# Both MLPs by seven products per 2x2 block, and a pooling mixer in ten overlapping tiles

## The chip, the cores and the metric

The kernel runs on one core of a Trainium2 chip, in fp32. TensorE multiplies, VectorE, ScalarE and GpSimd work element by element, SyncE issues most transfers. The metric is device time in microseconds; the kernel before took 2031.56 us (median of 3 runs, 2031.04 to 2033.41).

## The reference

One inference step of a two-layer decoder trunk, for a prompt of 1024 tokens behind 16 learned meta tokens, and for 8 samples of 4 tokens, which share the weights: 1072 tokens in all, 1024 channels.

```python
def sqrelu_mlp(x, w_up, w_down):
    return jnp.square(jax.nn.relu(x @ w_up)) @ w_down

# layer 0: h = rmsnorm(x); z = h @ w_in_even  -> gated short convolution (width 3)
#          and sliding-window attention with sinks -> concat @ w_out_even -> + x
# layer 1: h = rmsnorm(x); pool_mix(h): per channel group of 256 a trailing mean over
#          2 / 4 / 8 / 16 tokens minus h, times w_pool[group], times pool_scale -> + x
# both:    x = x + sqrelu_mlp(rmsnorm(x, norm_mlp[layer]), w_up[layer], w_down[layer])
```

`w_up` is 1024 x 4096 and `w_down` 4096 x 1024 per layer. The outputs are the activations of prompt and samples and the states of convolution, attention cache and pooling. The meta tokens are not needed after the mixer, so the second MLP works on 1056 tokens.

## The kernel before

Activations lie transposed in the state buffer: `xT` (named residual) holds 8 chunks of 128 channels by 1072 tokens. An fp32 product is made of three fp32r products: each operand is split into a high part (`_hi`, a copy on ScalarE) and a low part (`_lo`, a subtraction on VectorE), and `product` (L451 to L455) issues high x high, high x low and low x high into one PSUM bank. Columns are tokens in pieces of 368, 352 and 352; weights are the stationary 128 x 128 operand.

The stages follow one another: input projection, attention woven into the convolution's projections, the output projection in two halves of the contraction (`w_out_half`), the first MLP, the pooling mixer, the second MLP. An MLP runs over 8 groups of 512 hidden channels. In each group `up` makes 12 outputs of 24 matmuls, VectorE and ScalarE turn them into the hidden values (`relu`, `sq`, `hid_hi`, `hid_lo`) in the state buffer, and `down` makes 24 outputs of 12 matmuls, which VectorE adds to the residual (L1424). Four PSUM banks rotate. Weights come in steps of 512 KB through `raw` (two buffers) and are split into four slots of `w_hi` and `w_lo`.

The norm before an MLP needs a mean over channels: ScalarE squares, VectorE sums four chunks at a time (`norm_reduce`), a matmul sums over partitions, then root and reciprocal (`norm_rsqrt`). The up matmuls take the residual times the gain; `rs`, the factor per token, comes in with `relu`. So the matmuls of the first MLP do not wait for the norm. The mixer maps each of nine tiles of 128 tokens through `w_pool` (`map_tile`), scales the result (`z`), and makes the windows by a matmul with a band matrix (`window_tile`), one for the tile's own tokens and a second, 16 columns wide, for the tile before.

The order on each engine is the order in which the code is written; engines wait on one another by counting semaphores. GpSimd only issues transfers.

## Time and profile before

| | |
|---|---|
| median of 3 runs | 2031.56 us |
| profiled execution | 2034.41 us |
| its span, first to last instruction | 2032.6 us |
| first MLP | 447.6 to 1206.6 us |
| pooling mixer | 1206.6 to 1282.5 us |
| second MLP | 1282.5 to 2029.2 us |
| mean granted TensorE clock | 0.986 of full |

The profile's busy time of TensorE counts matmuls that overlap in the pipeline, so a matmul's mean duration is about twice the distance between two starts. What a stream of matmuls costs is read from the starts.

### The profile page before, as it was taken

Reading aid. Unit: us, or ns where it says so; the run is one execution under the profiler, and the core shown is the slowest. Engines: PE = TensorE matmul, PEld = TensorE weight load, DVE = VectorE, ACT = ScalarE, POOL = GpSimd, SP = SyncE. Lnnn points to the kernel's source line nnn. Section 1 sums busy time; section 2 is a strip of 40 time slices with the busy share of each in tenths; the row PEclk is TensorE's granted clock in tenths of the full one; section 3 lists DMA queues with packets and bytes.
Section 4 is the critical chain, followed back from the end, with each engine's and each line's share of the span. In section 5 each row is a group of like instructions: output and inputs, shape, how many; then the busy total and the mean of one; then the engine's idle time right before and its main releaser. Section 6 shows DMA issues by size and latency. Waiting matters only on the chain.

```text
span 2032.6 us, 30057 instructions
## 1 busy us (share of the span) xinstructions
PE 1989.8 (98%) x12287; PEld 1945.2 (96%) x12287; DVE 961.5 (47%) x1595; ACT 522.9 (26%) x929; POOL 36.2 (2%) x72
## 2 busy tenths in 40 slices
PE   5999999999999999999999999999999999999999
PEld 4888888999999999999999999999999999999999
DVE  5777775484333333333433477643433333334333
ACT  4323333143121221212131342312131212212120
POOL 1010000100000000000000000000000000000000
PEclk8899999999999999999999998899999999999999
DMA  5311101311111110211111110011111111112112
GB/s 178 84 49 32 32 32 59 99 42 61 43 42 42 41 55 28 62 31 51 52 42 51 43 42 5 21 52 53 52 40 53 41 41 41 41 41 62 31 53 86
DMA packets 134887, 102.01 MB, mean 50 GB/s; under 512 B 4481, under 2 KB 132657, under 8 KB 134784
## 3 DMA queue, kind: packets, MB, share of 16 engines
q1 hardware_dynamic: 130880, 90.52, 14.6%
q0 software_dynamic: 3648, 10.39, 1.7%
q8 instruction: 52, 0.85, 0.2%
q14 instruction: 19, 0.16, 0.0%
q10 hardware_dynamic: 288, 0.09, 0.0%
HBM read 95.17 MB, written 6.09 MB: 50 GB/s over the span
## 4 chain that ended last, share of the span: by engine, by line
PE 91%; DVE 5%; ACT 2%; issue 1%; DMA 1%; SPq 0%; DVEq 0%; ACTq 0%
PE out L453 29%; PE out L455 28%; PE out L454 28%; PE out L817 2%; PE turned L630 1%; DVE norm_sum L1158 1%; DVE head_sq L1214 1%; DMA raw<-in_w_in_even 1%; PE turned L613 1%; PE turned L509 1%; PE scores L579 1%; DVE w_lo L1148 0%; DVE act_lo L1181 0%; DVE rs L1173 0%; DVE conv_y L1367 0%
## 5 line engine op out<-in xcount | busy, mean ns | idle before, releaser
L453 PE MATMUL out<-act_hi,w_hi 128*128 128x352 f32 (+1 forms) x2160 | 718.0, 332 | 17.5 <-DVE act_lo L1181 10.0
L455 PE MATMUL out<-act_hi,w_lo 128*128 128x352 f32 (+1 forms) x2160 | 705.2, 326 | 0.0
L454 PE MATMUL out<-act_lo,w_hi 128*128 128x352 f32 (+1 forms) x2160 | 703.3, 326 | 0.0
L453 PE MATMUL out<-hid_hi,w_hi 128*128 128x352 f32 (+1 forms) x1536 | 501.1, 326 | 0.0
L455 PE MATMUL out<-hid_hi,w_lo 128*128 128x352 f32 (+1 forms) x1536 | 499.7, 325 | 0.0
L454 PE MATMUL out<-hid_lo,w_hi 128*128 128x352 f32 (+1 forms) x1536 | 497.6, 324 | 0.0
L453 PEld LDWEIGHTS out<-act_hi,w_hi 128*128 128x128 f32 x2160 | 410.0, 190 | 31.8 <-issue 22.0
L454 PEld LDWEIGHTS out<-act_lo,w_hi 128*128 128x128 f32 x2160 | 410.7, 190 | 2.0 <-issue 0.5
L455 PEld LDWEIGHTS out<-act_hi,w_lo 128*128 128x128 f32 x2160 | 410.1, 190 | 0.0
L1424 DVE TENSOR_TENSOR residual<-out,residual 128x352 f32<-128x352 f32 (+1 forms) x408 | 213.0, 526 | 397.9 <-PE out L455 397.6
L851 ACT ACTIVATE w_hi<-raw 128x1024 fp32r<-128x1024 f32 x156 | 161.2, 1052 | 642.6 <-PE out L455 635.2
L453 PEld LDWEIGHTS out<-hid_hi,w_hi 128*128 128x128 f32 x1536 | 289.0, 188 | 0.0
L454 PEld LDWEIGHTS out<-hid_lo,w_hi 128*128 128x128 f32 x1536 | 288.6, 188 | 0.0
L455 PEld LDWEIGHTS out<-hid_hi,w_lo 128*128 128x128 f32 x1536 | 287.9, 187 | 0.0
L1049 ACT ACTIVATE sq<-relu 128x352 f32<-128x352 f32 (+1 forms) x192 | 96.0, 500 | 509.5 <-DVE relu L1459 509.5
L1459 DVE SCALAR_TENSOR_TENSOR relu<-out,rs 128x352 f32<-128x352 f32 (+1 forms) x192 | 101.1, 527 | 260.2 <-PE out L455 260.0
L1148 DVE TENSOR_TENSOR w_lo<-raw,w_hi 128x1024 fp32r<-128x1024 f32 x156 | 188.2, 1223 | 69.3 <-ACT w_hi L851 69.2
L1465 DVE TENSOR_TENSOR hid_lo<-sq,hid_hi 128x352 fp32r<-128x352 f32 (+1 forms) x192 | 101.4, 528 | 212.0 <-ACT hid_hi L1051 212.0
L1051 ACT ACTIVATE hid_hi<-sq 128x352 fp32r<-128x352 f32 (+1 forms) x192 | 96.1, 501 | 6.1
L892 ACT ACTIVATE act_hi<-residual,prm 128x352 fp32r<-128x352 f32 (+1 forms) x96 | 49.6, 582 | 79.6 <-DVE residual L1424 54.7
L1158 DVE TENSOR_REDUCE norm_sum<-norm_buf 128x352 f32<-128x1408 f32 (+1 forms) x24 | 64.4, 2685 | 5.2 <-ACT norm_buf L868 5.0
L1181 DVE SCALAR_TENSOR_TENSOR act_lo<-residual,prm,act_hi 128x352 fp32r<-128x352 f32 (+1 forms) x96 | 50.1, 583 | 7.3 <-ACT act_hi L892 7.2
(135 smaller groups left out, 849.7 us busy)
## 6 DMA issues: line engine op xcount, KB each, us to landing
raw<-in_w_up SPq DMA_DIRECT2D x64, 512.0 KB, 4.1
raw<-in_w_down SPq DMA_DIRECT2D x64, 512.0 KB, 3.4
raw<-in_w_in_even SPq DMA_DIRECT2D x18, 512.0 KB, 3.7
out_y_cols<-residual SPq DMA_DIRECT2D x12, 352.0 KB, 2.4
raw<-in_w_out_even SPq DMA_DIRECT2D x8, 512.0 KB, 3.3
residual<-in_x_cols SPq DMA_DIRECT2D x8, 352.0 KB, 9.4
x_again<-in_x_cols POOLq DMA_DIRECT2D x16, 176.0 KB, 2.6
residual<-in_x_cols SPq DMA_DIRECT2D x4, 368.0 KB, 8.2
```

The costliest lines, as they stand in the source:

```text
L453: nc.tensor.matmul(out, lhs[0], rhs[0], start=first, stop=False)
L454: nc.tensor.matmul(out, lhs[0], rhs[1], start=False, stop=False)
L455: return nc.tensor.matmul(out, lhs[1], rhs[0], start=False, stop=last)
L851: nc.scalar.activation(w_hi[:, w % 4, :], raw[:, w % 2, :], ACT.Copy).then_inc(w_hi_done, 1)
L1049: nc.scalar.activation(sq[:, q % 2, 0:n], relu[:, q % 2, 0:n], ACT.Square).then_inc(hid_sq_done, 1)
L1051: nc.scalar.activation(hid_hi[p][:, chunk, 0:n], sq[:, q % 2, 0:n], ACT.Copy)\
L1148: nc.vector.tensor_tensor(w_lo[:, w % 4, :], raw[:, w % 2, :], f32(w_hi[:, w % 4, :]), ALU.subtract)\
L1158: nc.vector.tensor_reduce(total[:, half_, 0:c1 - c0], buf[:, :, 0:c1 - c0].rearrange("p c n -> p n c"), AX_X, ALU.add).then_inc(norm_summe ...
L1181: ins_ = nc.vector.scalar_tensor_tensor(out=act_lo[:, c, c0:c1], in0=xT[:, c, c0:c1], scalar=gain(n, c), in1=f32(act_hi[:, c, c0:c1]), op0 ...
L1424: nc.vector.tensor_tensor(xT[:, oc, c0:c1], out_bank[m % 4][:, 0:c1 - c0], xT[:, oc, c0:c1], ALU.add)\
L1459: nc.vector.scalar_tensor_tensor(out=relu[:, q % 2, 0:n], in0=out_bank[m % 4][:, 0:n], scalar=0.0, in1=rs[:, c0:c1], op0=ALU.max, op1=ALU. ...
L1465: nc.vector.tensor_tensor(hid_lo[p][:, chunk, 0:n], sq[:, q % 2, 0:n], f32(hid_hi[p][:, chunk, 0:n]), ALU.subtract).then_inc(hid_ready, 1)
```

## The change

**The MLPs.** The product of a 256 x 1024 weight block (transposed) with 1024 x all tokens is cut into 2 x 2 quadrants on either side: A11, A12, A21, A22 of 128 outputs by 512 contraction rows, and B11, B12, B21, B22 of 512 rows by half of the tokens (536, or 528 in the second MLP). Seven products take the place of eight:

```python
(A11, A12, S2, S1, S3, S4, A22) = range(7)      # left operands, in order of the products q
(B11, B21, T2, T1, T3, B22, T4) = range(7)      # right operands
# S1 = A21 + A22   S2 = S1 - A11   S3 = A11 - A21   S4 = A12 - S2
# T1 = B12 - B11   T2 = B22 - T1   T3 = B22 - B12   T4 = B21 - T2
```

A unit is one such block: 16 units make the hidden values of a layer (256 hidden channels each, full contraction), 16 more the down product (4 blocks of contraction, 4 of outputs). PSUM holds three accumulators of two banks; products 0, 2, 4 and 6 go on in one of them, 3 and 5 in another. On the way ScalarE copies partial results out (`keep_first`, `keep_sum`, `keep_fourth`), and VectorE adds them to the rest (`hidden11`, `hidden22`, `hidden12`); in the down units VectorE adds every product to the residual (`add_product`).

```diff
-def last_output(w, in_loop=False):
+UNITS, UPS = 32, 16
+NP = ((NT - 0) // 4, (NT - N_META) // 4)
+HALF_COLS = 2 * NP[0]
+STORED = (B11, B22, T1, T3, T2, B21, T4)
+R_SLOTS = 9
...
+            def one_product(U, q):
+                L, n = U // UNITS, block_no(U, q)
+                pe.wait_ge(left_ready, n + 1)
+                if first_use(U):
+                    pe.wait_ge(right_dve[q], hi_count(q, U) - (1 if q == T2 and U % UNITS == 0 else 0))
+                    if q != T2 or U % UNITS:
+                        pe.wait_ge(right_pool[q], pool_count(q, U))
...
+                elif q == 2:
+                    pe.wait_ge(acc_read[0], U + 1)
...
+                elif q == 4:
+                    pe.wait_ge(acc_read[2], U + 1)
+                elif q == 5:
+                    pe.wait_ge(acc_read[3], U + 1)
...
+                for piece in range(2):
+                    cols = slice(NP[L] * piece, NP[L] * (piece + 1))
+                    for k in range(4):
+                        lhs = [ring[:, slot, part, P * k:P * (k + 1)] for part in range(2)]
+                        rhs = [b_hi[q][:, k, cols], b_lo[q][:, k, cols]]
+                        begin = k == 0 and q in (0, 1, 3)
+                        ins_ = product(out[:, piece, :], lhs, rhs, begin, k == 3, q not in (0, 1, 3))
+                ins_.then_inc(products, 1)
```

**Left operands.** A weight block of 1 MB (`wide`, one buffer) is loaded per unit, after the last split of the unit before. GpSimd makes the sums; ScalarE and VectorE split the seven operands of 512 columns into a ring of nine slots. SyncE's wait for the next block, and GpSimd's sums:

```diff
+            def next_wide(U):
+                sp.wait_ge(left_ready, block_no(U, A22) + 1)
+                if U + 1 < 2 * UNITS:
+                    load_wide(U + 1)
...
+            def sum_of(U, q):
+                n = block_no(U, q)
+                pool.wait_ge(wide_in, 16 * wide_no(U))
+                if n >= R_SLOTS:
+                    pool.wait_ge(products, n - 8)
...
+                nc.gpsimd.tensor_tensor(dst, a, b, op).then_inc(sums_made, 1)
```

**Right operands.** The hidden values no longer stay in the state buffer. VectorE makes T1, T2, T3 and T4 of them too, all seven are stored to DRAM (`store_hidden`), and read back per 1024 hidden channels: in the last unit that uses an old set, each of the seven is loaded when its product is done (`load_right`), split high on ScalarE (`right_hi_part`), and low in two halves, on VectorE (`right_lo_part`) and GpSimd (`right_lo`). The upper half of the residual is kept in DRAM meanwhile (`keep_x`) and read back in the first down unit. `load_right` on SyncE, then the order of a unit on GpSimd, then on VectorE:

```diff
+            def load_right(U, r):
+                g = operand_set(U + 1) % 5 - 1
+                n = 2 * NP[U // UNITS]
+                sp.wait_ge(products, block_no(U, r) + 1)
...
+                sp.dma_start(b_full[r][:, :, 0:n], h_dram[STORED.index(r), :, 4 * g:4 * (g + 1), 0:n])\
+                    .then_inc(right_in[r], 16)
...
+            def unit(U):
+                for q in range(7):
+                    if last_use(U) and q >= 3:
+                        right_lo(q - 3, U + 1)
+                    if U % UNITS >= UPS and first_use(U) and q < 3:
+                        right_lo(q + 4, U)
+                    if q == 1 and U % UNITS < UNITS - 1:
+                        for s_ in (S1, S2, S3, S4):
+                            sum_of(U + 1, s_)
...
+            def unit(U):
+                if U % UNITS <= UPS:
+                    last_right(U - 1)
+                for q in range(7):
...
+                    else:
+                        add_product(U, q)
+                    if q == 0:
+                        late_lefts(U)
+                    next_lefts(U, q)
+                    if last_use(U) and q >= 3:
+                        right_lo_part(q - 3, U + 1)
+                    if U % UNITS >= UPS and first_use(U) and q < 3:
+                        right_lo_part(q + 4, U)
```

**The first unit of each MLP.** The right operands are now built from the normed residual (gain and `rs` are in before the products), in pieces of 268 tokens. The squares are summed one chunk at a time on GpSimd into `rs`. VectorE's order:

```diff
+            def first_unit(U):
...
+                first_rights(U, 2, T1)
+                first_rights(U, 2, T2)
+                first_rights(U, 2, T4)
+                invert(n, 3)
+                first_t2_lo(U, 2)
+                left_lo_part(U, S2)
+                normed(n, 3, 0)
+                first_rights(U, 3, T1)
+                normed(n, 3, 1)
+                first_rights(U, 3, T2)
+                first_rights(U, 3, T4)
+                first_t2_lo(U, 3)
+                left_lo_part(U, S1)
+                right_lo_part(T1, U)
+                late_lefts(U)
+                right_lo_part(T3, U)
+                hidden11(U)
```

**The mixer.** Ten tiles of 105 or 106 tokens, each mapped with the 15 tokens before it, so that one band of up to 106 columns per group makes its windows and the second matmul is gone. `pool_scale` is multiplied into `w_pool` once on GpSimd; ScalarE scales `z`; VectorE adds a half tile in one instruction instead of four.

```diff
-TILES = [(c0 + P * i, min(c0 + P * (i + 1), c1)) for c0, c1 in PIECES for i in range(3)]
+TILE_STARTS = ((16, 122, 228, 334, 439, 544), (544, 650, 756, 862, 968, NT))
+TILES = [(h[i], h[i + 1]) for h in TILE_STARTS for i in range(5)]
...
+                        ins_ = nc.tensor.matmul(out[:, at_:at_ + n], own, band[0:rows_, BAND_W * gi:BAND_W * gi + n],
+                                                start=True, stop=True)
```

The second half of the output projection has four pieces of 268 tokens instead of three.

Three places in the engines' queues. TensorE inside the first MLP, before, where a down output begins (`hid_hi`, `hid_lo` are hidden values, `w_hi` weights):

```order
L453 MATMUL out<-hid_hi_86,w_hi 128x352 [waits out_freed,hid_ready]
L454 MATMUL out<-hid_lo_87,w_hi 128x352
L455 MATMUL out<-hid_hi_86,w_lo 128x352
L453 MATMUL out<-hid_hi_86,w_hi 128x352
L454 MATMUL out<-hid_lo_87,w_hi 128x352
```

And TensorE now, at the start of the sixth product of the first unit (`ring` holds the left operands, `b_hi` and `b_lo` the right ones, `turned` is the second accumulator):

```order
L789 MATMUL out<-b_lo_102,ring 128x268
L790 MATMUL out<-b_hi_101,ring 128x268
L788 MATMUL turned<-b_hi_105,ring 128x268 [waits acc_read3,left_ready]
L789 MATMUL turned<-b_lo_106,ring 128x268
L790 MATMUL turned<-b_hi_105,ring 128x268
```

The stream is of the same three matmuls with fewer columns, 24 to a wait. (The profile adds waits on right operands where a set is first used.)

GpSimd before, from the output projection to the end:

```order
L432 DMA x_again<-in_x_cols 128x352 [waits out_freed] x16
L440 DMA pool_state<-in_pool_cols 128x960 [waits stored_pool,norm_summed,out_freed]
L441 DMA band<-in_bands 128x960
L379 DMA out_pool_prompt<-tail_rows 15x1024 [waits pool_copied]
L379 DMA out_pool_sample<-tail_rows 4x1024 x8
```

GpSimd now, at the first replacement of the right operands (`b_lo` from `b_full` and `b_hi` are low halves, `ring_full` from `wide` are sums of weight blocks):

```order
L700 TENSOR_TENSOR b_lo_98<-b_full_99,b_hi_97 128x1072 [waits right_hi3]
L700 TENSOR_TENSOR b_lo_102<-b_full_103,b_hi_101 128x1072 [waits right_hi4]
L700 TENSOR_TENSOR b_lo_106<-b_full_107,b_hi_105 128x1072 [waits right_hi5]
L693 TENSOR_TENSOR ring_full<-wide 128x512 [waits products,wide_in]
L693 TENSOR_TENSOR ring_full<-ring_full,wide 128x512 [waits sums_made,products,wide_in]
L693 TENSOR_TENSOR ring_full<-wide 128x512 [waits products,wide_in]
L693 TENSOR_TENSOR ring_full<-wide,ring_full 128x512 [waits sums_made,products,wide_in]
L700 TENSOR_TENSOR b_lo_110<-b_full_111,b_hi_109 128x1072 [waits right_hi6]
```

Where GpSimd issued transfers it now computes, and four sums for the following unit stand between the sixth and the seventh low half.

VectorE before, at the start of the first MLP:

```order
L1181 SCALAR_TENSOR_TENSOR act_lo<-residual,prm,act_hi 128x352 [waits norm_hi]
L1181 SCALAR_TENSOR_TENSOR act_lo<-residual,prm,act_hi 128x352
L1158 TENSOR_REDUCE norm_sum<-norm_buf 128x352 [waits norm_mean,norm_sq]
L1459 SCALAR_TENSOR_TENSOR relu<-out,rs 128x368 [waits out_ready]
L1465 TENSOR_TENSOR hid_lo_85<-sq,hid_hi_84 128x368 [waits hid_hi_done]
L1459 SCALAR_TENSOR_TENSOR relu<-out,rs 128x368 [waits out_ready]
L1465 TENSOR_TENSOR hid_lo_85<-sq,hid_hi_84 128x368 [waits hid_hi_done]
```

VectorE now, between the first product and the last pieces of T2 (`b_full` and `b_spare` hold normed values and the combinations made of them):

```order
L1975 TENSOR_TENSOR b_full_99<-b_spare_100,b_full_99 128x4x268 [waits xn_made]
L1934 SCALAR_TENSOR_TENSOR b_spare_112<-residual,prm,rs 128x268 [waits dve_step]
L1934 SCALAR_TENSOR_TENSOR b_spare_112<-residual,prm,rs 128x268 x3
L1978 TENSOR_TENSOR b_full_95<-b_spare_112,b_full_99 128x4x268 [waits xn_made]
L1981 TENSOR_TENSOR b_full_111<-b_full_111,b_full_95 128x4x268 [waits t2_made]
L1966 TENSOR_TENSOR b_lo_94<-b_full_95,b_hi_93 128x4x268 [waits right_hi2,dve_step]
```

Norm and combinations stand in one row ahead of the third product, where before the last sum of squares was followed by the hidden values of the first outputs.

## Rows read from the trace of the kernel before

**Rows 1.** The page's head: span and busy time of each engine
```profile
span 2032.6 us, 30057 instructions
PE 1989.8 (98%) x12287; PEld 1945.2 (96%) x12287; DVE 961.5 (47%) x1595; ACT 522.9 (26%) x929; POOL 36.2 (2%) x72
```

**Rows 2.** The page's chain that ended last, by engine and by line
```profile
PE 91%; DVE 5%; ACT 2%; issue 1%; DMA 1%; SPq 0%; DVEq 0%; ACTq 0%
PE out L453 29%; PE out L455 28%; PE out L454 28%; PE out L817 2%; PE turned L630 1%; DVE norm_sum L1158 1%; DVE head_sq L1214 1%; DMA raw<-in_w_in_even 1%; PE turned L613 1%; PE turned L509 1%; PE scores L579 1%; DVE w_lo L1148 0%; DVE act_lo L1181 0%; DVE rs L1173 0%; DVE conv_y L1367 0%
```

**Rows 3.** Waits of TensorE from 300 us on: total, times, longest
```profile
PE turned L509 <- DVE norm_sum L1158: 1.1, 1, 1.1
...
PE out L453 <- DVE z L1522: 0.3, 1, 0.3
```

**Rows 4.** Windows: length, busy time by engine, clock, DMA share, GB/s
```profile
447.60:1206.60 759.00, 759.00 (x4654) 758.06 (x4653) 308.73 (x483) 182.23 (x291) 1.07 (x2) 1.00 0.15 46
1206.60:1282.50 75.90, 74.51 (x554) 72.99 (x553) 61.66 (x134) 25.35 (x42) 4.50 (x9) 0.86 0.07 17
1282.50:2029.20 746.70, 746.70 (x4614) 745.81 (x4612) 284.36 (x457) 160.58 (x259) 0.00 (x0) 1.00 0.16 48
```

**Rows 5.** Timeline of TensorE: ends of 47 starts (352 columns), 26 (368)
```profile
1189.83 0.32 PE L453 MATMUL out<-hid_hi,w_hi 128*128 128x352 f32 x1
...
1197.29 0.32 PE L454 MATMUL out<-hid_lo,w_hi 128*128 128x352 f32 x1
599.68 0.33 PE L453 MATMUL out<-hid_hi,w_hi 128*128 128x368 f32 x1
...
603.89 0.33 PE L454 MATMUL out<-hid_lo,w_hi 128*128 128x368 f32 x1
```

**Rows 6.** The same, 256 columns: ends of 42 starts, and of 13 at half clock
```profile
1206.62 0.28 PE L453 MATMUL out<-w_hi,act_hi 128*128 128x256 f32 x1
...
1211.43 0.28 PE L455 MATMUL out<-w_hi,act_lo 128*128 128x256 f32 x1
...
1230.87 0.41 PE L453 MATMUL out<-w_hi,act_hi 128*128 128x256 f32 x1
...
1233.43 0.32 PE L453 MATMUL out<-w_hi,act_hi 128*128 128x256 f32 x1
```

**Rows 7.** VectorE groups by form: busy, mean ns of one, idle before
```profile
L1148 DVE TENSOR_TENSOR w_lo<-raw,w_hi 128x1024 fp32r<-128x1024 f32 x156 | 188.2, 1223 | 69.3 <-ACT w_hi L851 69.2
L1424 DVE TENSOR_TENSOR residual<-out,residual 128x352 f32<-128x352 f32 x336 | 174.9, 523 | 336.9 <-PE out L455 336.6
L1181 DVE SCALAR_TENSOR_TENSOR act_lo<-residual,prm,act_hi 128x352 fp32r<-128x352 f32 x72 | 37.1, 579 | 4.7 <-ACT act_hi L892 4.6
L1385 DVE TENSOR_TENSOR act_lo<-conv_out,act_hi 128x1408 fp32r<-128x1408 f32 x2 | 3.2, 1622 | 0.0
L1173 DVE RECIPROCAL rs<-rs 128x352 f32<-128x352 f32 x7 | 16.4, 2349 | 0.0
L1173 DVE RECIPROCAL rs<-rs 128x368 f32<-128x368 f32 x2 | 4.9, 2446 | 4.9 <-ACT rs L883 4.9
```

**Rows 8.** ScalarE groups by form
```profile
L851 ACT ACTIVATE w_hi<-raw 128x1024 fp32r<-128x1024 f32 x156 | 161.2, 1052 | 642.6 <-PE out L455 635.2 <-DMA raw<-in_w_in_even 7.3
L1049 ACT ACTIVATE sq<-relu 128x352 f32<-128x352 f32 x160 | 79.6, 498 | 427.1 <-DVE relu L1459 427.1
L868 ACT ACTIVATE norm_buf<-residual 128x1408 f32<-128x1408 f32 x18 | 24.7, 1371 | 28.9 <-DVE norm_sum L1158 28.9
```

**Rows 9.** GpSimd groups by form: the largest, and a memset
```profile
L432 POOL DMA_DIRECT2D x_again<-in_x_cols x24 | 12.9, 540 | 254.7 <-DVE xa_sb L1350 222.8 <-DVE residual L1416 30.6 <-DMA out_v_sample<-v_blocks 1.4
L1598 POOL MEMSET const-float32-0.0<- 128x1 f32 x1 | 0.1, 99 | 0.3 <-issue 0.3
```

**Rows 10.** A DMA issue (KB, us to landing), and windows at the start
```profile
raw<-in_w_down SPq DMA_DIRECT2D x64, 512.0 KB, 3.4
...
12.00:16.00 4.00, 3.83 (x12) 3.83 (x13) 3.79 (x6) 2.35 (x3) 0.00 (x0) 1.00 1.07 428
20.00:25.00 5.00, 0.33 (x1) 0.36 (x2) 3.87 (x2) 1.85 (x2) 0.00 (x0) 0.68 1.04 357
```

**Rows 11.** A window tile in TensorE's timeline, and a window at half clock
```profile
1235.41 3.64 PE L817 MATMUL out<-band,z 128*128 128x128 f32 x32
...
1272.00:1282.00 10.00, 10.00 (x45) 9.50 (x45) 8.52 (x18) 5.12 (x8) 0.00 (x0) 0.50 0.00 0
```

**Rows 12.** The end: last matmul and last add in the timeline
```profile
2028.96 0.32 PE L455 MATMUL out<-hid_hi,w_lo 128*128 128x352 f32 x1
...
2029.31 0.53 DVE L1424 TENSOR_TENSOR residual<-out,residual 128x352 f32<-128x352 f32 x1 [1.43 <-PE out L455]
```

More of the change, by code:

```diff
@@ L374, in _ @@
+            sp.wait_ge(stored_sp, 16 * 7)
         @block.gpsimd
@@ L446, in _, with add_square, add_piece @@
-            pool.wait_ge(stored_pool, 16 * n_stored[0])
+            def add_square(k, c0, c1, begin):
+                pool.wait_ge(sum_begun, begin + 1)
+                pool.wait_ge(squared, k + 1)
+                if k:
+                    pool.wait_ge(added, k)
+                nc.gpsimd.tensor_tensor(rs[:, c0:c1], rs[:, c0:c1], square_view(k, c1 - c0), ALU.add).then_inc(added, 1)
+            def add_piece(n, p, first=0, end=7):
+                c0, c1 = NORM_PIECES[n][p]
+                for i in range(first, end):
+                    add_square(add_no(n, p) + i, c0, c1, begun_no(n, p))
@@ L449, in _, with product @@
+            first_rights(UNITS)
+            for U in range(UNITS, 2 * UNITS):
+                unit(U)
         @block.tensor
         def _(pe):
[L451 to L455 removed]
+            def product(out, lhs, rhs, first, last, resumed=False):
+                skip = resumed
+                nc.tensor.matmul(out, lhs[0], rhs[0], start=first, stop=False, skip_group_check=skip)
+                nc.tensor.matmul(out, lhs[0], rhs[1], start=False, stop=False, skip_group_check=skip)
+                return nc.tensor.matmul(out, lhs[1], rhs[0], start=False, stop=last, skip_group_check=skip)
@@ new lines, in normed @@
+            def normed(n, p, high):
+                c0, c1, x0, x1 = piece_cols(n, p)
+                dst = (b_full if p < 2 else b_spare)[T4 if high else T1]
+                for k in range(4):
+                    c = 4 * high + k
+                    ins_ = nc.vector.scalar_tensor_tensor(out=dst[:, k, x0:x1], in0=xT[:, c, c0:c1], scalar=gain(n, c),
+                                                          in1=rs[:, c0:c1], op0=ALU.mult, op1=ALU.mult)
+                ins_.then_inc(xn_made, 1)
@@ L1562, in _ @@
[L1562 to L1578 removed]
+                    x = xT[:, 4 * half_:4 * half_ + 4, a:b]
```

1509 lines of the change are left out of this document (965 added, 544 removed).

## The prediction, made before the changed kernel was run

> **What bounds the kernel now.** I read the head of the page first. The span is 2032.6 us and TensorE is busy for 98% of it, VectorE for 47%, ScalarE for 26%, GpSimd for 2% [rows 1]. A matmul's busy time overlaps its neighbour's, so this alone does not say that TensorE sets the time. The chain that ended last does: 91% of it lies on TensorE, 85% on the three matmuls of the helper `product` [rows 2]. The waits agree: after 300 us the longest wait of any TensorE line is 1.1 us [rows 3]. Then the stretches: the first MLP fills 447.6 to 1206.6 us (759.0), the pooling mixer 75.9, the second MLP 1282.5 to 2029.2 (746.7) [rows 4]. In both MLPs VectorE works 40% of the time and the DMA queues 15 to 16%. So the time of an MLP is its count of matmuls by the distance from one start to the next, and the other engines have room that the change wants to use.
>
> That distance comes from starts, not from the mean duration of 0.32 us. 352 columns: 7.46 us over 46 distances, 0.162; at other places 0.161. 368 columns: 4.21 us over 25, 0.168 [rows 5]. 256 columns in the pooling mixer: 4.81 us over 41, 0.1173; at the granted half clock (1.2 GHz) 2.56 us over 12, 0.213 [rows 6]. Check: 4608 matmuls per MLP (8 groups, 36 outputs, 576 matmuls), a third with 368 columns, give 1536 x 0.168 + 3072 x 0.161 = 752.6 us, and 6 us of norm and state matmuls lie between them: 759. The second has 352 throughout: 4608 x 0.161 = 742. Both fit.
>
> **The matmuls.** A unit is 256 output rows, 1024 contraction rows and all tokens: 7 products of 2 pieces, 4 chunks and 3 matmuls, 168 in all, of 268 columns in the first MLP and 264 in the second. 32 units make 5376 matmuls per MLP, 17% more than 4608, each a quarter shorter. Columns fall by one eighth. From 256 to 352 columns the distance grows by 0.0437 us, so 268 columns take 0.1173 + 12/96 x 0.0437 = 0.1228 us and 264 take 0.1209. The streams are 660.2 and 650.0 us. Weight loads stay 128 columns wide, and beside 256 columns they did not hold the stream up [rows 6], so I add nothing for them. A product is 2.95 us, a unit 20.6 us.
>
> **What the other engines must do in 20.6 us.** VectorE: 512 columns of tensor_tensor are 0.69 us and 536 are 0.72 (from 0.523 at 352 and 1.223 at 1024); 1072 are 1.27 (1.62 at 1408 less 336 columns at 1.04 ns) [rows 7]. An up unit has 7 splits and 10 operations on hidden values: 12.0 us. A down unit has 7 splits and 7 adds, 9.9 us. ScalarE: 512 columns 0.63 us, 536 0.65, 2144 1.97 [rows 8]; an up unit is 7.7 us. Both are hidden under TensorE, and in an ordinary unit each result has one product of slack. GpSimd gets four 512-column sums per unit and half of each new right operand's low part. No row shows GpSimd computing on a tensor: its rows are DMA issues and memsets of 0.1 us [rows 9]. The bounds from the nearest rows are VectorE's tensor_tensor, 1.04 ns a column, and its slowest elementwise operation, the reciprocal, 6.06 ns (97 ns for 16 columns) [rows 7]. I take 2.3 ns, near their geometric middle: 1.3 us for 512 columns, 2.6 us for 1072. Transfers: a 1 MB weight block needs 3 us at the 357 to 428 GB/s that the queues moved when full, and 512 KB took 3.4 us to landing, of which some 1.9 is latency [rows 10]; so 4.9 us. Per up unit 1 MB comes and 1.9 MB goes, about a third of what the queues can move. Cost of all this in ordinary units: nothing, covered by TensorE.
>
> The Trainium skill ("GPSIMD Engine Reference", 3.1) gives 4497 ns for 2048 fp32 columns, 1.96 times VectorE. By that estimate the two prices would be 1.3 and 2.5 us and the sum would stay; no row here shows it.
>
> **The operand changes.** Eight times (after each 16 up units and after down units 4, 8 and 12, in each MLP) all seven right operands are replaced: read back from DRAM (1.1 MB each, 3 us when the queues are full, the pace of one product), split high on ScalarE, and low in halves on VectorE and GpSimd. Count from the start of the last unit that uses the old ones. Product r frees slot r at 2.95(r+1); the new one is due at 20.6 + 2.95 r. GpSimd first needs the next weight block (lands 10.7) and makes four sums (15.9), then six low halves (31.5). In its queue four more sums stand before the seventh half, and their weights land only at about 32.8, since SyncE may load them once VectorE has split the previous ones at 27.9. So sums to 38.0, seventh half to 40.6, due at 38.4: 2.3 us late. VectorE's order puts `add_product` of the third and fourth product behind low halves of operands that have just landed; they finish within 1.5 us of when TensorE wants the banks, so some of that shows too. I take 4 us for six of the changes. The two after the up units also have the last hidden values to finish (five operations after the sixth product, 3.6 us, then `last_right` ahead of the first add) and the residual read back: 8 us. Together 40 us. Bounds: nothing, and 15 us each (below).
>
> **The first unit of each MLP.** Before, the norm lay beside the matmuls of other pieces. Now the first unit needs seven right operands built from the normed residual, and its order on VectorE is serial. With 268 columns: normed chunk 0.49 us, reciprocal 1.84, each combination of 4 x 268 columns 1.27 [rows 7]. From the end of the output projection: the adds and norm of piece 2 still queued, 4.2 us, hold the first product; T1, T2, T4 of piece 2, reciprocal, T2's low part and S2's split let the third product begin at 14.2 instead of 10.2; its second piece waits for two norms, T1, T2, T4 and a low part, to 23.4; the fourth, fifth and seventh products wait for low parts from GpSimd at 27.8, 32.5 and 39.4. The unit ends at about 42 us instead of 20.6: 21.7 lost, and some 3 more because TensorE's clock falls in such gaps, as it does in the mixer before, where 256 columns took 0.213 us after the thin window matmuls [rows 6, 11]. 25 us. The second MLP starts from pieces of 318 and 210 columns and must wait for the squares and GpSimd sums of the last piece (7 x 0.6 us) before its second product: 33 us.
>
> **The mixer.** Now 75.9 us. Ten tiles instead of nine: 240 map matmuls of 256 columns, 28 us. A window tile was 16 matmuls in 3.64 us [rows 11]; now it is 8 of 106 columns and no second band, 1.8 us, 18 in all. The states and norms are 5. At its head the last unit's adds, squares and row norms (about 7 steps, GpSimd among them) keep the first window back to 11 us, with two maps beside them. 58 us; bounds 51 (no wait) and 76 (as before).
>
> **Sum**, against the profiled execution's own 2034.4 us (its span and 1.8 outside): 447.6 before the MLP, unchanged in work; 660.2 + 25; 58; 650.0 + 33; 40 for the changes; 5.2 from the last matmul to the end, as before [rows 12]. That is 1919.0. The runs' median stands 2.8 us below the profiled execution, so 1917.
>
> **Rivals.** (A) Everything is covered: no operand change shows and the first units lose 15 us together instead of 58. 1917 - 40 - 43 = 1834, with half of it 1875. For it: the idle shares in rows 4. Against: the serial order of the first units, which only far shorter operations would undo. (B) VectorE and GpSimd take turns. No row has both computing at once. If one waits for the other whenever VectorE reads two tensors of the state buffer, 16.5 us of splits interleave with 28.6 us of GpSimd work in 28 us at each operand change; by alternating them in queue order I get 15 us per change, and 10 more in each first unit: 1917 + 80 + 20 = 2017. Ordinary units stay covered (10 + 5 us of 20.6). (C) The other side: GpSimd's price per column. Between the landing at 10.7 and the due time of the seventh operand it has eight sums and seven halves, 3.0 us + 11600 columns at p ns. At p = 2.3 that is the forecast; when p passes 3.7, each change costs over 18 us and the gain is gone; at 4.5 each costs 27, 1877 + 216 = 2093, slower than before. The bound of 6.06 allows it; that adding is simpler than a reciprocal speaks against it. A kernel that does not make the products it says is excluded by the instruction order, which has 168 matmuls per unit.
>
> The Trainium skill ("SBUF — State Buffer", "Who interferes with whom") says that VectorE and GpSimd share a port pair, and that a VectorE instruction with two state-buffer inputs and a GpSimd instruction that reads there exclude one another for the whole instruction. By that rule (B) would come true, 2017 us; no run here shows it yet.
>
> **Chances.** Forecast, 1885 to 1965 us: 0.55. A, below 1885: 0.12. B, 1965 to 2045: 0.25. C, above: 0.08. Less than 0.2% (4 us) is what a measurement of this kernel can't tell from no change. Faster takes the forecast, A and most of B: 0.88; same 0.03; slower C and B's top: 0.09. The range is 1870 to 2020: it leaves out half of A and the tops of B and C, and holds the bounds of the operand changes (0 to 15 us each) with the first units as taken. The likeliest case's own range is 1885 to 1965.
>
> **What would show it.** Starts of matmuls with 268 columns 0.123 us apart in an ordinary unit. A GpSimd sum near 1.3 us, and 2.6 for 1072 columns; the same next to VectorE splits as alone (against B). TensorE's waits gathered at eight places, ended by GpSimd's low half or the adds, 4 to 8 us each; the first units 42 to 49 us long; the mixer near 58. The prediction is wrong if ordinary units are longer than 20.6 us, if distances stay near 0.16, or if the waits at operand changes end in transfers.

## The result: slower, 2071 us, and the profile after

The changed kernel took 2070.84 us (median of 4 runs, 2070.28 to 2073.79), the kernel before 2031.36 us beside it: 1.020 times, interval 1.0187 to 1.0213. The prediction was faster, 1917 us, within 1870 to 2020. The profiled execution took 2073.8 us, 2072.0 of them span.

The page's head answers to [rows 1], its chain to [rows 2]:

```profile
span 2072.0 us, 33448 instructions
PE 1842.2 (89%) x13797; PEld 1791.8 (86%) x13797; DVE 1308.9 (63%) x1703; ACT 678.1 (33%) x1121; POOL 666.8 (32%) x461
...
PE 64%; DVE 17%; DMA 6%; issue 5%; POOL 4%; ACT 2%; SPq 0%; POOLq 0%; DVEq 0%; ACTq 0%
```

TensorE is busy for 148 us less, but now it stands still for 230 us where it was 43. The chain has left it: 21% lies on VectorE and GpSimd. The three stretches answer to [rows 4]; the columns are the same (length, busy time by engine, clock, DMA share, GB/s):

```profile
443.40:1218.40 775.00, 689.18 (x5379) 684.62 (x5379) 491.25 (x561) 253.97 (x368) 308.19 (x183) 0.94 0.36 129
1218.40:1289.20 70.80, 62.52 (x476) 60.84 (x474) 40.63 (x69) 35.28 (x63) 19.16 (x20) 0.90 0.13 43
1289.20:2068.60 779.40, 687.32 (x5380) 682.66 (x5380) 479.32 (x554) 240.60 (x353) 287.18 (x175) 0.93 0.36 129
```

Both MLPs are longer than before (759.0 and 746.7), though 5376 matmuls of 268 columns need only 665 us. Some of TensorE's longest waits (total, times, longest) answer to [rows 3], where the longest was 1.1 us:

```profile
PE out L788 <- DVE residual L2035: 59.1, 8, 10.1
PE out L788 <- POOL b_lo L700: 32.1, 13, 4.5
PE scores L788 <- DVE ring L1944: 26.3, 10, 10.4
PE out L788 <- DVE ring L1944: 15.7, 2, 10.9
...
PE out L788 <- DVE residual L1917: 12.1, 1, 12.1
```

L2035 is `add_product`, L1944 and L700 are the low parts of a weight block and of a right operand (GpSimd's half), L1917 belongs to the first unit. Each of the eight operand changes has one of the eight waits on `residual`; at the two changes after the up units a longer one, 6.2 and 10.4 us, ends with L1944. First a stretch of 260 us without a wait, then one of the changes, in the first MLP, in windows of 20 us:

```profile
520.00:780.00 260.00, 260.00 (x2105) 260.00 (x2105) 156.01 (x216) 84.58 (x150) 65.05 (x50) 1.00 0.40 142
...
880.00:900.00 20.00, 20.00 (x164) 20.00 (x163) 9.76 (x14) 4.09 (x7) 5.10 (x4) 1.00 0.17 54
900.00:920.00 20.00, 20.00 (x164) 20.00 (x164) 12.04 (x14) 5.50 (x4) 7.39 (x5) 1.00 0.74 286
920.00:940.00 20.00, 9.27 (x70) 8.86 (x70) 20.00 (x11) 11.78 (x11) 17.25 (x6) 0.85 0.37 151
940.00:960.00 20.00, 17.23 (x124) 17.04 (x124) 11.84 (x13) 4.09 (x7) 7.95 (x5) 0.90 0.17 54
```

A window counts every matmul that reaches into it, two more than start there where the stream is whole. So in the first row the starts lie 0.1236 us apart (264 columns, 1400 to 1640 us: 0.1221). At 880 us all is nearly as forecast: no wait, VectorE works half the time, GpSimd a quarter. From 920 us VectorE is busy without a gap and gets 11 instructions done where 14 took 9.76 us. Between 900 and 960 us 352 matmuls start, so this change lost 60 - 352 x 0.1236 = 16.5 us. Counted in this way the eight lost 21.6, 16.5, 15.7, 14.9, and 24.3, 17.6, 16.5, 14.9 us in the second MLP: 142 us where 40 were forecast.

Not all of it is waiting. TensorE's waits in these eight stretches add up to 109 us, 13.5 of them here. From 933.9 to 944.2 us, late in the long wait and behind it, the granted clock is at half (1.2 GHz; as means of the windows 0.85 and 0.90), and matmuls start 0.22 us apart instead of 0.12:

```profile
939.51 0.43 PE L789 MATMUL out<-b_lo,ring 128*128 128x268 f32 x1
939.73 0.43 PE L790 MATMUL out<-b_hi,ring 128*128 128x268 f32 x1
```

246 matmuls in the eight stretches start at this distance, which makes about 24 us. The forecast put nothing for the clock there.

What VectorE and GpSimd did there (start, duration, instruction):

```profile
917.51 1.78 DVE L1944 TENSOR_TENSOR ring<-wide,ring 128x512 fp32r<-128x512 f32 x1 [0.47 <-ACT ring L1388]
919.22 3.58 DVE L1959 TENSOR_TENSOR b_lo<-b_full,b_hi 128x1072 fp32r<-128x1072 f32 x1
922.72 0.70 DVE L2035 TENSOR_TENSOR residual<-turned,residual 128x536 f32<-128x536 f32 x1
923.35 2.38 DVE L1944 TENSOR_TENSOR ring<-wide,ring 128x512 fp32r<-128x512 f32 x1
925.65 3.58 DVE L1959 TENSOR_TENSOR b_lo<-b_full,b_hi 128x1072 fp32r<-128x1072 f32 x1
929.16 0.70 DVE L2035 TENSOR_TENSOR residual<-out,residual 128x536 f32<-128x536 f32 x1
929.78 5.16 DVE L1944 TENSOR_TENSOR ring<-ring_full,ring 128x512 fp32r<-128x512 f32 x2
934.87 3.51 DVE L1959 TENSOR_TENSOR b_lo<-b_full,b_hi 128x1072 fp32r<-128x1072 f32 x1
...
938.93 1.28 DVE L1944 TENSOR_TENSOR ring<-ring_full,ring 128x512 fp32r<-128x512 f32 x2
...
940.73 1.26 DVE L1959 TENSOR_TENSOR b_lo<-b_full,b_hi 128x1072 fp32r<-128x1072 f32 x1
```

```profile
918.71 18.53 POOL L700 TENSOR_TENSOR b_lo<-b_full,b_hi 128x1072 fp32r<-128x1072 f32 x6
947.85 1.30 POOL L693 TENSOR_TENSOR ring_full<-wide 128x512 f32<-128x512 f32 x1 [10.61 <-DMA wide<-in_w_down]
...
953.52 2.45 POOL L700 TENSOR_TENSOR b_lo<-b_full,b_hi 128x1072 fp32r<-128x1072 f32 x1
```

While GpSimd makes its six halves (918.7 to 937.2 us), VectorE's low half takes 3.5 us and its 512-column split 2.4 to 2.6; once GpSimd stops, the same instructions take 1.26 and 0.64. The adds between them, which read one input from PSUM, stay at 0.70. GpSimd's own prices are near the assumed ones: 1.30 us for 512 columns, 2.45 for 1072; the six halves beside VectorE took 3.09 each. Its seventh half comes at 953.5 us, behind four sums that waited for their weights.

### The profile page after: what moved, and what is told of

It is laid out like the page before. It is cut to its first block, busy times and chain, and to the rows that moved or that the text cites. A ratio compares the mean times of both kernels' runs of the same rounds, so it can differ in the third digit from the quotient of the medians.

```text
span 2072.0 us, 33448 instructions
## 1 busy us (share of the span) xinstructions
PE 1842.2 (89%) x13797; PEld 1791.8 (86%) x13797; DVE 1308.9 (63%) x1703; ACT 678.1 (33%) x1121; POOL 666.8 (32%) x461
## 4 chain that ended last, share of the span: by engine, by line
PE 64%; DVE 17%; DMA 6%; issue 5%; POOL 4%; ACT 2%; SPq 0%; POOLq 0%; DVEq 0%; ACTq 0%
PE out L788 14%; PE out L790 13%; PE out L789 13%; PE turned L790 4%; PE turned L789 4%; PE turned L788 4%; DVE b_lo L1959 4%; DVE ring L1944 4%; DMA b_full<-h_dram 3%; PE scores L788 2%; PE scores L789 2%; PE scores L790 2%; DMA wide<-in_w_down 2%; POOL b_lo L700 2%; POOL ring_full L693 2%
## 5 line engine op out<-in xcount | busy, mean ns | idle before, releaser
L788 PE MATMUL out<-b_hi,ring 128*128 128x268 f32 (+1 forms) x2048 | 602.2, 294 | 145.1 <-DVE residual L2035 59.1
L789 PE MATMUL out<-b_lo,ring 128*128 128x268 f32 (+1 forms) x2048 | 599.6, 293 | 0.0
L790 PE MATMUL out<-b_hi,ring 128*128 128x268 f32 (+1 forms) x2048 | 598.8, 292 | 0.0
L788 PEld LDWEIGHTS out<-b_hi,ring 128*128 128x128 f32 x2048 | 400.7, 196 | 150.9 <-issue 120.4
L789 PEld LDWEIGHTS out<-b_lo,ring 128*128 128x128 f32 x2048 | 400.6, 196 | 0.0
L790 PEld LDWEIGHTS out<-b_hi,ring 128*128 128x128 f32 x2048 | 400.2, 195 | 0.0
L788 PE MATMUL turned<-b_hi,ring 128*128 128x268 f32 (+1 forms) x1024 | 293.9, 287 | 3.9 <-issue 2.9
L789 PE MATMUL turned<-b_lo,ring 128*128 128x268 f32 (+1 forms) x1024 | 293.8, 287 | 0.0
L790 PE MATMUL turned<-b_hi,ring 128*128 128x268 f32 (+1 forms) x1024 | 293.4, 287 | 0.0
L788 PE MATMUL out<-act_hi,w_hi 128*128 128x352 f32 (+2 forms) x656 | 221.0, 337 | 18.6 <-DVE act_lo L1679 8.8
L2035 DVE TENSOR_TENSOR residual<-out,residual 128x536 f32<-128x536 f32 (+1 forms) x128 | 90.9, 710 | 200.7 <-PE out L790 200.3
L790 PE MATMUL out<-act_hi,w_lo 128*128 128x352 f32 (+2 forms) x656 | 211.0, 322 | 0.0
L789 PE MATMUL out<-act_lo,w_hi 128*128 128x352 f32 (+2 forms) x656 | 210.9, 321 | 0.0
L700 POOL TENSOR_TENSOR b_lo<-b_full,b_hi 128x1072 fp32r<-128x1072 f32 (+1 forms) x66 | 196.3, 2999 | 24.0 <-ACT b_hi L1430 24.0
L1944 DVE TENSOR_TENSOR ring<-ring_full,ring 128x512 fp32r<-128x512 f32 x256 | 190.4, 784 | 20.1 <-ACT ring L1388 20.0
L1944 DVE TENSOR_TENSOR ring<-wide,ring 128x512 fp32r<-128x512 f32 x192 | 195.2, 1017 | 11.7 <-ACT ring L1388 10.7
L788 PEld LDWEIGHTS turned<-b_hi,ring 128*128 128x128 f32 x1024 | 194.3, 190 | 4.9 <-issue 4.9
L790 PEld LDWEIGHTS turned<-b_hi,ring 128*128 128x128 f32 x1024 | 194.5, 190 | 0.0
```

The source lines that it names most:

```text
L700: nc.gpsimd.tensor_tensor(b_lo[r][:, 2:4, 0:n], src[:, 2:4, 0:n], b_hi[r][:, 2:4, 0:n].bitcast(F32), ALU.subtract).then_inc(right_pool[r], 1)
L788: nc.tensor.matmul(out, lhs[0], rhs[0], start=first, stop=False, skip_group_check=skip)
L789: nc.tensor.matmul(out, lhs[0], rhs[1], start=False, stop=False, skip_group_check=skip)
L790: return nc.tensor.matmul(out, lhs[1], rhs[0], start=False, stop=last, skip_group_check=skip)
L1944: nc.vector.tensor_tensor(cells(ring, n, 1), left_source(U, q), f32(cells(ring, n, 0)), ALU.subtract)\
L2035: nc.vector.tensor_tensor(x, acc_view(q, U), x, ALU.add).then_inc(acc_read[q], 1)
```

## Experiments

Three theories were tested. **T**: an instruction of VectorE whose inputs all lie in the state buffer and one of GpSimd that works there take turns, so that their times add. **Q**: GpSimd's own queue (six halves, four sums, the seventh half) is the late party, whatever VectorE does. **D**: the operands come back from DRAM too late (a load took 7.7 to 8.1 us to landing, 4.9 were assumed).

| Kernel | us | to before |
|---|---|---|
| changed kernel | 2070.8 | 1.020 (1.0187 to 1.0213) |
| seventh half ahead of the sums | 2053.9 | 1.011 (1.0087 to 1.0133) |
| GpSimd's halves alone (one run) | 2039.6 | |
| GpSimd a quarter, VectorE the rest | 2026.9 | 0.9974 (0.9957 to 0.9991) |
| VectorE whole low parts | 1992.4 | 0.9811 (0.9787 to 0.9835) |
| the same, spread | 1991.5 | 0.9816 (0.9799 to 0.9833) |
| and in the first units | 1977.0 | 0.9746 (0.9728 to 0.9764) |
| the same, sums later | 1977.3 | 0.9733 (0.9702 to 0.9763) |
| and VectorE the weight sums | 1970.9 | 0.9704 (0.9672 to 0.9735) |
| with sums and spread | 1970.2 | 0.9714 (0.9695 to 0.9732) |
| VectorE's halves alone (one run) | 1945.4 | |

### VectorE makes the whole low part at a change

```diff
-                    if last_use(U) and q >= 3:
-                        right_lo(q - 3, U + 1)
...
-                nc.vector.tensor_tensor(b_lo[r][:, 0:2, 0:n], src[:, 0:2, 0:n], f32(b_hi[r][:, 0:2, 0:n]), ALU.subtract)\
+                end = 4 if U % UNITS else 2
+                nc.vector.tensor_tensor(b_lo[r][:, 0:end, 0:n], src[:, 0:end, 0:n], f32(b_hi[r][:, 0:end, 0:n]), ALU.subtract)\
```

`right_lo` is GpSimd's half.

> At the eight operand changes VectorE makes the whole low part of a right operand (2144 columns, 2.39 us by its own rate), GpSimd none. First units as they are. Theory T (VectorE and GpSimd take turns): the work that must be done one after the other falls from 3.7 us (1.27 + 2.45) to 2.39 per operand, and only the weight sums still collide; a change costs some 7 us instead of 17.7 (141 us over eight in the changed kernel), so about 1985. Theory Q (GpSimd's own queue makes the seventh operand late, no turns): GpSimd is free, the waits on its low halves (32 us) go, about 2040. Theory D (the operands land too late from DRAM): 2070, no change.

1992.4 us. T's figure was missed by 7 us, Q's and D's by 48 and 78. Taking work from the half idle GpSimd and giving it to VectorE, the engine that is late, made the kernel 78 us faster, and faster than the kernel before.

### One half left out

Each of these two kernels leaves out one engine's half at the changes, and TensorE takes the high part in its place, so that it has as many matmuls. The cut is of the first kernel; chunks 2 and 3 are GpSimd's half, and (0, 1) stands in the other, VectorE's.

```diff
-                        rhs = [b_hi[q][:, k, cols], b_lo[q][:, k, cols]]
+                        low = b_hi if k in (2, 3) and operand_set(U) % 5 else b_lo
+                        rhs = [b_hi[q][:, k, cols], low[q][:, k, cols]]
```

Without GpSimd's:

> Leaves out GpSimd's half of the low parts at the operand changes (TensorE takes the high part in their place); VectorE's half stays. Theory T: VectorE's 1072 columns cost 1.27 us unless one of GpSimd's sums runs, a change costs 2 to 4 us, about 1950. Theory Q: the same time, so it does not tell T from Q, but Q has VectorE's durations unchanged at 2.1 us. Theory D: 2060 to 2070.

1945.4 us. The change at 900 us is gone, with the loads as they were (their share of the queues still 0.79):

```profile
900.00:920.00 20.00, 20.00 (x164) 20.00 (x163) 18.64 (x21) 15.60 (x14) 4.10 (x4) 1.00 0.79 311
920.00:940.00 20.00, 20.00 (x164) 20.00 (x163) 9.29 (x14) 4.92 (x9) 6.36 (x5) 1.00 0.16 53
```

D falls: with the same transfers TensorE waits for nothing there, and the clock stays at 1.00. Of the other seven changes only the two after the up units still have waits, 4.2 and 4.7 us.

Without VectorE's:

> Leaves out VectorE's half of the low parts at the operand changes (TensorE takes the high part in their place, so as many matmuls); GpSimd's half and queue stay. Theory T: VectorE's seven 1072-column operations were the ones that waited for GpSimd and held the adds and splits behind them; without them about 7 us per change remain, 1985. GpSimd's 1072 columns cost 2.45 us where no VectorE operation on two tensors of the state buffer runs. Theory Q: little changes, 2050 to 2070. Theory D: 2070.

2039.6 us: T missed by 55, Q's range began 10 higher. GpSimd's trace shows why T's figure was too low:

```profile
912.03 17.08 POOL L700 TENSOR_TENSOR b_lo<-b_full,b_hi 128x1072 fp32r<-128x1072 f32 x6
935.58 1.29 POOL L693 TENSOR_TENSOR ring_full<-wide 128x512 f32<-128x512 f32 x1 [6.46 <-DMA wide<-in_w_down]
...
941.43 2.44 POOL L700 TENSOR_TENSOR b_lo<-b_full,b_hi 128x1072 fp32r<-128x1072 f32 x1
```

Even without VectorE's halves the seventh half comes last, behind sums that wait 6.46 us for their weights. TensorE waits for it once at each change, 3.1 to 6.2 us, 42 us in all. So Q is true of a part. How much that is in the changed kernel, the next one tells.

### The seventh half ahead of the four sums

```diff
-                    if q == 1 and U % UNITS < UNITS - 1:
+                    if q == (2 if U % UNITS >= UPS and first_use(U) else 1) and U % UNITS < UNITS - 1:
```

> Only GpSimd's order changes: at an operand change its seventh low half stands before the four weight sums of the next unit, not behind them. Theory T: the last waits of a change, on GpSimd's low half (32 us over 13 waits in the changed kernel), shrink to about 10 us, while the waits on VectorE's adds (59 us) stay: about 2050. Theory Q: all that an operand change costs beyond 2 us goes: 1960. Theory D: 2070.

2053.9 us where T had 2050; 17 us gained, 2.1 a change. Waits on GpSimd's low half fell from 32.1 to 13.5 us, those on VectorE's add stayed:

```profile
PE out L788 <- DVE residual L2035: 62.1, 10, 10.1
```

### Taking turns measured by itself

Behind the last store of the changed kernel, each engine alone and both at once. A phase gives the number of instructions of VectorE and of GpSimd, and the next one starts when both are done. `two` and GpSimd's `d`, `a`, `b` have 2 x 528 columns, `d1` and `a1` 528, and `acc_x` lies in PSUM.

```diff
+            for phase, (nv, ng) in enumerate(((7, 0), (0, 7), (7, 7), (14, 0), (14, 7), (14, 0), (14, 7), (0, 7), (7, 7))):
...
+                            ins_ = nc.vector.tensor_tensor(two[0], two[1], two[2], ALU.subtract)
...
+                            ins_ = nc.vector.tensor_tensor(d1, acc_x[0][:, :, 0:NP[1]], a1, ALU.subtract)
...
+                            ins_ = nc.vector.tensor_copy(d1, a1)
...
+                            ins_ = nc.gpsimd.tensor_tensor(d, a, b, ALU.subtract)
...
+                            ins_ = nc.gpsimd.tensor_copy(d, a)
```

> The changed kernel with a measurement put behind its last store: seven subtractions of 2 x 528 columns with two state-buffer inputs by VectorE alone, seven by GpSimd alone, seven by each at once; then VectorE's adds with one PSUM input (2 x 264 columns, 14) alone and beside seven GpSimd subtractions; VectorE's one-input copies (14) alone and beside them; GpSimd's copies alone and beside VectorE's two-input subtractions. Taking turns: both at once take the sum of the two alone, about 7 x (1.25 + 2.45) = 26 us, and a VectorE instruction is stretched from 1.25 to 2.5 us or more; the adds with a PSUM input stay at 0.71 us beside GpSimd. Rival, the stretch in the changed kernel came from waits or from the transfers beside it and not from the two engines: both at once take the longer of the two, 17 us, and VectorE's stay at 1.25 us. What the copies do beside GpSimd is open in both.

VectorE's groups and GpSimd's (busy us, mean ns of one). Alone: L464, L470, L474; L482, L490. At once: L466 with L484, L472 with L486, L476 with L488, L468 with L492.

```profile
L466 DVE TENSOR_TENSOR b_lo<-b_hi,b_hi 128x1056 fp32r<-128x1056 f32 x7 | 21.5, 3144 | 16.9 <-POOL b_lo L482 16.9
L476 DVE CAST b_lo<-b_hi 128x528 fp32r<-128x528 f32 x14 | 20.4, 1530 | 0.0
L468 DVE TENSOR_TENSOR b_lo<-b_hi,b_hi 128x1056 fp32r<-128x1056 f32 x7 | 13.5, 1991 | 7.3 <-POOL b_lo L490 7.3
L472 DVE TENSOR_TENSOR b_lo<-out,b_hi 128x528 fp32r<-128x528 f32 x14 | 8.7, 698 | 0.0
L470 DVE TENSOR_TENSOR b_lo<-out,b_hi 128x528 fp32r<-128x528 f32 x14 | 8.7, 696 | 2.4 <-POOL b_lo L484 2.4
L464 DVE TENSOR_TENSOR b_lo<-b_hi,b_hi 128x1056 fp32r<-128x1056 f32 x7 | 8.3, 1254 | 2.1 <-DMA out_y_cols<-residual 2.1
L474 DVE CAST b_lo<-b_hi 128x528 fp32r<-128x528 f32 x14 | 4.9, 428 | 8.3 <-POOL b_lo L486 8.3
```

```profile
L484 POOL TENSOR_TENSOR b_lo<-b_hi,b_hi 128x1056 fp32r<-128x1056 f32 x7 | 23.8, 3431 | 0.1
L488 POOL TENSOR_TENSOR b_lo<-b_hi,b_hi 128x1056 fp32r<-128x1056 f32 x7 | 17.9, 2583 | 5.2 <-DVE b_lo L474 5.2
L486 POOL TENSOR_TENSOR b_lo<-b_hi,b_hi 128x1056 fp32r<-128x1056 f32 x7 | 16.6, 2420 | 9.0 <-DVE b_lo L470 9.0
L482 POOL TENSOR_TENSOR b_lo<-b_hi,b_hi 128x1056 fp32r<-128x1056 f32 x7 | 16.6, 2408 | 36.3 <-issue 36.3
L492 POOL CAST b_lo<-b_hi 128x1056 fp32r<-128x1056 f32 x7 | 14.4, 2101 | 0.1
L490 POOL CAST b_lo<-b_hi 128x1056 fp32r<-128x1056 f32 x7 | 7.1, 1069 | 2.4 <-DVE b_lo L476 2.4
```

VectorE alone 8.3 us, GpSimd alone 16.6; at once GpSimd needs 23.8, nearly the sum of 24.9, and VectorE's instruction is stretched from 1254 to 3144 ns. With one input in PSUM nothing changes: 696 and 698 ns, GpSimd 2408 and 2420. VectorE's copies pay too, 4.9 us alone and 20.4 beside GpSimd, and so does a GpSimd copy, 7.1 and 14.4. This is T, without transfers or TensorE. The Trainium skill ("SBUF — State Buffer", "Who interferes with whom") has such an exclusion for VectorE instructions with two state-buffer inputs and for copies in a mode that takes both ports, and none for those with at most one state-buffer input outside such a mode. The trace agrees: two inputs and copies were stretched (1254 to 3144 and 428 to 1530 ns), the form with a PSUM input was not.

### GpSimd a quarter, VectorE three quarters

```diff
-                nc.gpsimd.tensor_tensor(b_lo[r][:, 2:4, 0:n], src[:, 2:4, 0:n], b_hi[r][:, 2:4, 0:n].bitcast(F32),
+                k = 3 if U % UNITS else 2
+                nc.gpsimd.tensor_tensor(b_lo[r][:, k:4, 0:n], src[:, k:4, 0:n], b_hi[r][:, k:4, 0:n].bitcast(F32),
```

> The changed kernel with another share at the eight changes: VectorE makes three quarters of a low part (1608 columns, about 1.80 us alone) and GpSimd a quarter (536, about 1.25 us); the first units as in the changed kernel. Taking turns: a low part takes the sum of both, 3.05 us, against 3.72 in the changed kernel (2071 us) and 2.39 where VectorE makes it whole (1992 us), so the time lies between these two, by the line through them (79 us for 1.33 us of 56 low parts) at 2030 us. Rival, GpSimd's small share is fitted beside VectorE's adds with a PSUM input, which it doesn't touch, and takes 0.59 us of each low part off VectorE: 56 x 0.59 = 33 us less than 1992, 1959 us.

2026.9 us: T's 2030, and not the rival's 1959. The time follows the two engines' time added up: 3.72 us per low part gave 2071 us, 3.05 gave 2027, 2.39 gave 1992, and 1.27 (GpSimd's half left out) 1945. The kernel with GpSimd's halves alone does not lie on this line: 2.45 us per low part, and 2040 us, since there the late seventh half comes on top. Of the shares tried (a half, a quarter, none) none of GpSimd's paid; its column costs 2.29 ns and VectorE's 1.18.

### VectorE makes the low parts of the first units too

```diff
-                end = 4 if U % UNITS else 2
+                end = 4
...
-                right_lo(T1, U)
```

The last line is one of GpSimd's six halves, which all go; the cut is against the kernel with VectorE's whole low parts at the changes.

> As the kernel in which VectorE makes the whole low part at the eight changes (1992 us), and in the first unit of each MLP too: GpSimd's six low halves there are VectorE's. Taking turns: six times 2.45 us of GpSimd that kept VectorE out become six times 1.27 us of VectorE; about 7 us less for each MLP, so 1975 to 1985 us. Rival, VectorE's own chain of work is what the first unit waits for and GpSimd's halves lay beside it: six times 1.27 us more in each MLP, 2000 to 2008 us.

1977.0 us, 15.4 less, as T has it. TensorE's wait before the first product of the first MLP fell from 12.11 to 6.78 us (two rows, of the changed kernel and of this one):

```profile
455.54 0.56 PE L788 MATMUL out<-b_hi,ring 128*128 128x268 f32 x1 [12.11 <-DVE residual L1917]
```

```profile
453.09 0.56 PE L776 MATMUL out<-b_hi,ring 128*128 128x268 f32 x1 [6.78 <-DVE residual L1902]
```

### A change spread over more products

```diff
+CHANGE_AT = (3, 4, 6, 7, 9, 10, 11)
-                    if last_use(U) and q >= 3:
-                        right_lo_part(q - 3, U + 1)
+                    if last_use(U) and q in CHANGE_AT:
+                        right_lo_part(CHANGE_AT.index(q), U + 1)
```

> As the kernel in which VectorE makes the whole low part at the eight changes (1992 us), but with the seven high and low parts of a change put behind the products 3, 4, 6, 7, 9, 10, 11 in place of 3 to 9 (counted from the first product of the last unit before the change). What is left of a change there is VectorE's amount of work: 7 x 2.39 of low parts, 7 x 0.70 of adds, 7 x 0.68 of weight parts are 26 us in 20.6 us. Spread over nine products it is 29.5 us in 26.5: 3 us of loss in place of 5.9, 24 us less, 1965 to 1972 us. Rival, the loss comes from operands that are ready too late, and later places make it more: 2000 us and above.

1991.5 us: 24 us were expected, none came, and the rival's loss did not come either. VectorE works there almost without a gap from 903.85 to 936.4 us. The trace shows what took the place of the old waits: the seventh low part, now last, falls beside GpSimd's sums for the following unit, takes 3.48 us instead of 2.37, and TensorE waits 1.91 us for it:

```profile
931.25 3.48 DVE L1957 TENSOR_TENSOR b_lo<-b_full,b_hi 128x2144 fp32r<-128x2144 f32 x1
```

So it is at all eight changes, 1.9 us each time. But the kernel without GpSimd's sums does not gain by the spread either (1970.2 against 1970.9 below), so the sums are not the whole reason; the rest is open.

### The sums after a change later, and by VectorE

```diff
+                        if U % UNITS >= UPS and first_use(U):
+                            pool.wait_ge(products, block_no(U, 3) + 1)
```

> As the kernel in which VectorE makes all low parts, first units too (1977 us), but GpSimd's four weight sums of the first unit after each change start after that unit's fourth product, past the change, and not in the middle of it. Taking turns: they stretched VectorE's instructions there by about 3 us a change (3.48 and 2.85 us for low parts of 2.38), which goes: 1977 less up to 24 us, 1953 to 1965 us. Rival, the sums are wanted right after and come late: 1977 to 2000 us.

1977.3 us, no gain: the added wait moved nothing. At the change at 900 us those sums start at 923.07 us without it, when their weights land, and at 922.63 with it. So this run says nothing for or against T. The row with the wait, then the one without:

```profile
922.63 3.20 POOL L693 TENSOR_TENSOR ring_full<-wide 128x512 f32<-128x512 f32 x1 [18.44 <-PE turned L780]
```

```profile
923.07 3.18 POOL L693 TENSOR_TENSOR ring_full<-wide 128x512 f32<-128x512 f32 x1 [18.46 <-DMA wide<-in_w_down]
```

Then the sums by VectorE (`nc.gpsimd.tensor_tensor(dst, a, b, op)` becomes `nc.vector.tensor_tensor(dst, a, b, op)` behind the fourth to sixth product), with the spread and without:

> As the kernel with the spread changes and VectorE making the low parts of the first units whole, and with the four weight sums of a unit made by VectorE too (from unit 2 of each MLP on), so that GpSimd has next to nothing in the MLPs. Taking turns: four sums of 1.3 us of GpSimd beside a change kept VectorE out for up to 5.2 us, and cost VectorE 2.8 us now; with the other two steps 1945 to 1960 us. Rival, GpSimd's sums lay in gaps of VectorE and are worth having there: each change gets 2.8 us longer, 1975 to 1985 us.

> As the kernel in which VectorE makes all low parts (1977 us), and the four weight sums of a unit too (from unit 2 of each MLP on), but with the parts of a change at their places behind products 3 to 9: the kernel that made 1970 us without its spread. The spread alone had moved nothing (1991.5 against 1992.4), so by itself the move of the sums to VectorE should give that kernel's 7 us: 1966 to 1972 us. Rival, with GpSimd silent a spread of VectorE's work counts after all, since no sums fall into the longer stretch any more: the kernel without it is then 10 us or more slower, 1980 us and above.

1970.2 and 1970.9 us. The first lies 10 us above T's range, the second within the one that followed from it. The sums bring 6 us, less than thought. At 0.970 to 0.971 of the time before, these are the fastest kernels here that compute everything.

## Why the prediction was wrong, point by point

**Right, or nearly.** The distance of the matmuls: 0.1228 and 0.1209 us were forecast, 0.1236 and 0.1221 measured, 11 us over both MLPs. Ordinary units have no waits, and seven products take 20.8 us where 20.6 were forecast. GpSimd's prices, 1.3 and 2.6 us, measured 1.30 and 2.45, so rival C falls. VectorE's 1.27 and 0.72 hold when GpSimd is silent (1.26 and 0.72). The end took the 5.2 us.

**Wrong: the operand changes, 40 us, measured 142.** This is the step that failed. It laid VectorE's halves and splits beside GpSimd's halves at their prices alone, and looked only for the instruction that comes last, as if the two engines worked side by side. Their times add. Between the first low part and the seventh, VectorE has 7 x 1.27 + 7 x 0.69 = 13.7 us of state-buffer work and GpSimd 7 x 2.45 + 8 x 1.30 = 27.6: 41 us of work that excludes one another, due within about 20.6 us and a product or two of slack. Without GpSimd's halves 125 us went, 15.7 a change (one run). The late seventh half, which the prediction did see at 2.3 us, is 2.1 of them by the swapped order. The other 13 to 14 are the turns with what follows from them. The lower clock behind the waits is among it, 3 us a change, a term that the forecast had at nothing; so are the waits for GpSimd's first half at the two changes after the up units (4.5 and 3.1 us), which no run separates. What stays without GpSimd's halves is mostly at the two changes after the up units, some 5 us each. The loads landed 3 us later than assumed, which cost nothing that shows in the run without GpSimd's halves.

**Too small: the first units, 25 + 33 us.** What is left of each MLP when the stream at its measured distance and the changes are taken off: 775.0 - 664.6 - 68.7 = 41.7, and 779.4 - 656.6 - 73.4 = 49.4. Of the 33 us too many, GpSimd's low halves are 15 by experiment. The first product waited 12.1 us where 4.2 were forecast. Four norm instructions there took 4.40 us beside GpSimd and 1.71 without it:

```profile
448.01 4.40 DVE L1934 SCALAR_TENSOR_TENSOR b_spare<-residual,prm,rs 128x268 f32<-128x268 f32 x4
...
468.54 1.71 DVE L1934 SCALAR_TENSOR_TENSOR b_spare<-residual,prm,rs 128x268 f32<-128x268 f32 x4
```

The lower clock counts here as well: 62 and 87 matmuls started 0.22 us apart, which makes 6 and 9 us where the forecast named some 3. GpSimd's norm adds and its third right operand were not moved in any run; how the other 18 us divide between them, VectorE's longer chain and the clock is open.

**The mixer, 58 us, measured 70.8.** The 7 us for the wait at its head (58 against the bound of 51) came true: three waits there are 7.0 us. Some 5 us more is the clock, granted at 0.61 to 0.74 over the first 21.6 us, during and behind these waits:

```profile
1218.40:1230.00 11.60, 4.64 (x25) 3.97 (x24) 10.15 (x11) 3.38 (x6) 4.97 (x3) 0.74 0.00 1
1230.00:1240.00 10.00, 10.00 (x59) 10.00 (x58) 3.58 (x14) 4.43 (x10) 0.00 (x0) 0.61 0.06 21
```

The window matmuls took 22 us where 18 were forecast, and the states and norms 9 where 5 were, part of that at the lower clock. No run tested this part alone. Before the MLP the kernel is 4 us shorter than forecast.

**The rivals.** B was the mechanism, with 0.25. Its price of 15 us a change is close to the waits (109 us over eight, 13.6 each); it lacked the lower clock behind them, and 17.8 were lost. In each first unit it had 10 us more than the forecast where some 17 came on top, and nothing in the mixer; 2017 against 2071. No row showed both engines computing at once [rows 9], so the forecast's cover at the changes was an assumption, and it deserved no more weight than B. And 15 us a change, found by alternating the two queues, was no upper bound: six of the eight lost more, the first of each MLP 21.6 and 24.3.

Sum of the errors: 11 for the matmuls' distance, 102, 33 and 13 for changes, first units and mixer, less 4 before the MLP, make 155 us; with the 1919 of the profiled execution that is 2074, and it took 2073.8.
